# Gathering the first expert pair's tokens by products with the selection matrix, and adding the sample shift on GpSimd

## The chip, the cores and the metric

The kernel runs on one core of a Trainium2 chip, as one launch. The metric is the device time in microseconds; the median of three runs is compared. The engines are PE (TensorE, matrix products), DVE (VectorE), ACT (ScalarE), POOL (GpSimd) and SP (SyncE, which here only issues DMAs).

## The reference, cut to what matters

One decoder layer is computed in float32 for 256 prompt tokens and 8 sample tokens, 1024 features each. The first half (attention, a state space branch, their merge and `w_o`) gives a new `x`. The second half is the one that the change touches:

```python
h2 = rms_norm(x, w['g_norm2']) * (1 + sc2) + sh2
x = x + gt2 * grouped_moe(h2, w_router, b_router, w['w_gate'], w['w_up'], w['w_down'])

def grouped_moe(h, w_router, b_router, w_gate, w_up, w_down):
    logits = (t @ w_router).astype(f32) + b_router.astype(f32)   # 16 experts in 4 groups
    probs = jax.nn.softmax(logits, axis=-1)
    ...                                                          # best group, then top 2 in it
    act = jax.nn.silu(jnp.einsum('td,edf->tef', t, w_gate)) * jnp.einsum('td,edf->tef', t, w_up)
    act = act * comb.astype(act.dtype)[..., None]
    y = jnp.einsum('tef,efd->td', act, w_down)
```

`sc2` and `sh2` (scale and shift) come from the conditions: one pair for all prompt tokens, one for each of the 8 samples. Each expert has three matrices of 1024 x 512 or 512 x 1024 float32, 2.1 MB each.

## The kernel before, in words

The program is written by hand for each engine, with semaphores between them. A list `jobs` sets the order of PE's work for the first half; ACT and DVE walk the same list and read each job's PSUM bank (`filled`, `release`, `read_out`).

Near the end of the list stand the jobs `o` (the product with `w_o`, 8 of them), `lg` (router logits and sums of squares), `hx` and `rk`. `hx` turns the normed features, kept as feature x token, into rows of tokens: three blocks `a` of 128, 128 and 8 tokens (`TOK`), each in two halves `f` of 512 features. ACT copies them out of PSUM with the row's factor `rstd` into `h2tok[a]`, and stores them to DRAM (`h2_d`). The shift of the prompt is added much later, when ACT copies gathered tokens (`gathered`, with bias `shq`). As that adds the prompt's shift to samples too, the rows of the samples must carry the difference of the two shifts, `shrow`. Before the change PE does this: for `a` = 2 it multiplies by `ident` and adds a product of `sdiag` (the deviation on a diagonal) with `shrow` in the same bank. `rk` ranks the tokens of each expert by bf16 products of the assignment, from which DVE's `select` builds the selection matrix `sel` of a pair of experts (264 tokens in three blocks by 128 places, 64 for each expert).

The experts are computed in 8 pairs `j`. For each pair PE gives token numbers (`ids`), from which DVE makes row numbers `idx`; POOL fetches these rows from `h2_d` by an indirect DMA into `xrow` (`fetch`); PE flips them to feature x place (`turn`); ACT copies them to `xg` (`gathered`); then come `gate_up`, `turn_act`, `down` and `combine`. `first_wts` gives the weights of the places for pair 0. `gate_up` has 32 products, in the order gate first half, gate second half, up first half, up second half.

SP streams the expert matrices as 96 halves of 1.05 MB (`load_half(m)`, m = 0 to 95) through 18 places in SBUF. Places 0 to 15 become free during the first half of the layer. Place 16 lies in `attT`, which holds `shrow`, and place 17 in `work`, which holds `h2tok[2]`. From m = 18 on, SP waits until the place of m - 18 is used up (`freed`): `gate_half` for m = 18 and 19, then `gate_done`, `up_half`, `up_done`, `down_half` and `down_done`. SP executes in order, so a wait holds all later loads.

## Time and profile before

| | us |
|---|---|
| median of 3 runs | 853.85 (851.89 to 855.59) |
| the profiled execution's own time | 847.97 |
| its span | 846.4 |
| PE busy | 780.7 (92%) |
| DVE busy | 364.7 (43%) |
| ACT busy | 304.5 (36%) |
| POOL busy | 98.5 (12%) |
| mean DMA rate over the span | 260 GB/s |
| mean granted PE clock | 0.968 of full speed |

### The profile page before, as it was taken

The page shows a single profiled execution, that of the slowest core. Times are in us where ns is not written, and L with a number is a line of the kernel's source. Part 1 is how long each engine was busy: PE and PEld are TensorE (multiplying, and loading weights), DVE is VectorE, ACT ScalarE, POOL GpSimd, SP SyncE. Part 2 cuts the span into 40 slices and gives each one's busy share as a digit, 9 for nine tenths or more (in the row PEclk, how much of TensorE's full clock was granted, in tenths as well). Part 3 has the DMA queues.
Part 4 walks back from the last instruction along what each step waited for, and adds up shares of the span by engine and source line. Part 5 has one row for each costly group of instructions (what it writes and reads, how often), then busy time and mean ns, then how long its engine had stood idle before and what let it go on. Part 6 is the DMA issues. An engine that isn't in the chain of part 4 may idle for free.

```text
span 846.4 us, 12511 instructions
## 1 busy us (share of the span) xinstructions
PE 780.7 (92%) x4573; PEld 546.0 (65%) x4573; DVE 364.7 (43%) x845; ACT 304.5 (36%) x733; POOL 98.5 (12%) x156
## 2 busy tenths in 40 slices
PE   3798979999999899898999999999779999999997
PEld 3375757787776687677887778888534444344434
DVE  3355636675675066375999511112301232222203
ACT  1223216675566256463977100101312222112213
POOL 4321021121200212512001100000010000000000
PEclk9899989999999999999999989999779999999999
DMA  9796353778675712227998995562859999999992
GB/s 294 245 353 216 100 162 118 260 231 299 208 274 180 244 39 78 87 70 212 403 279 255 358 357 183 158 240 100 305 190 423 420 421 420 422 419 421 422 419 97
DMA packets 93532, 219.68 MB, mean 260 GB/s; under 512 B 11792, under 2 KB 67672, under 8 KB 78980
## 3 DMA queue, kind: packets, MB, share of 16 engines
q1 hardware_dynamic: 78850, 181.71, 59.0%
q0 software_dynamic: 7984, 31.87, 11.4%
q10 hardware_dynamic: 6634, 5.25, 2.0%
q8 instruction: 39, 0.64, 0.3%
q14 instruction: 25, 0.20, 0.1%
HBM read 207.58 MB, written 13.22 MB: 261 GB/s over the span
## 4 chain that ended last, share of the span: by engine, by line
PE 66%; DMA 11%; SPq 9%; ACT 5%; DVE 3%; issue 3%; POOL 1%; POOLq 1%; ACTq 0%; DVEq 0%
PE bank L1622 17%; PE bank L1927 9%; PE bank L1848 7%; SPq L549 5%; PE bank L1949 5%; PE bank L1555 4%; DMA out_ssm_sample<-arena 4%; PE bank L1856 4%; PE bank L1618 3%; DMA arena<-in_w_down 3%; PE bank L1830 3%; PE bank L1968 2%; SPq L530 2%; PE bank L1678 2%; DMA out_k_prompt<-arena 1%
## 5 line engine op out<-in xcount | busy, mean ns | idle before, releaser
L1622 PE MATMUL bank<-h_normed,weight_ring 128*128 128x264 f32 x1024 | 243.2, 395 | 10.1 <-ACT arena L894 6.0
L1622 PEld LDWEIGHTS bank<-h_normed,weight_ring 128*128 128x128 f32 x1024 | 195.3, 194 | 48.1 <-ACT arena L894 6.4
L1927 PE MATMUL bank<-arena,h_normed 128*64 128x512 f32 x176 | 79.0, 603 | 0.0
L1848 PE MATMUL bank<-y_T,weight_ring 128*128 128x264 f32 x256 | 58.7, 392 | 0.0
L1927 PE MATMUL bank<-weight_ring,h_normed 128*64 128x512 f32 x192 | 56.3, 594 | 0.6 <-ACT h_normed L1031 0.6
L1848 PEld LDWEIGHTS bank<-y_T,weight_ring 128*128 128x128 f32 x256 | 49.4, 194 | 8.6
L1488 DVE SCALAR_TENSOR_TENSOR x_residual<-bank,modulation,x_residual 128x256 f32<-128x256 f32 x64 | 28.8, 484 | 57.9 <-PE bank L1968 57.9
L1481 DVE TENSOR_TENSOR arena<-arena,bank 128x512 f32<-128x512 f32 x8 | 8.7, 1087 | 104.5 <-PE bank L1927 104.5
L1555 PE MATMUL bank<-identity,arena 128*128 128x128 f32 (+5 forms) x236 | 32.2, 277 | 16.7 <-ACT arena L830 9.3
L1555 PEld LDWEIGHTS bank<-identity,arena 128*128 128x128 f32 (+5 forms) x236 | 26.7, 148 | 27.8 <-issue 22.8
L981 ACT ACTIVATE arena<-conv_out,expanded 128x128 f32<-128x128 f32 x128 | 38.3, 388 | 12.7 <-DVE arena L1364 11.7
L1927 PEld LDWEIGHTS bank<-weight_ring,h_normed 128*64 128x64 f32 x192 | 17.5, 137 | 35.8 <-issue 34.8
L1949 PE MATMUL bank<-arena 128*64 128x512 f32 x88 | 39.2, 595 | 0.0
L799 POOL DMA_INDIRECT h_normed<-h_scratch,token_rows x8 | 8.3, 1033 | 263.5 <-DVE token_rows L1449 143.3
L1287 DVE SCALAR_TENSOR_TENSOR conv_work<-conv_work,vectors 128x288 f32<-128x288 f32 x72 | 37.6, 523 | 2.5
L1031 ACT ACTIVATE h_normed<-bank,conv_tails 128x128 f32<-128x128 f32 x64 | 17.4, 382 | 58.9 <-PE bank L1555 58.9
L1927 PEld LDWEIGHTS bank<-arena,h_normed 128*64 128x64 f32 x176 | 24.1, 139 | 13.8 <-issue 13.8
L1927 PE MATMUL bank<-conv_out,h_normed 128*64 128x512 f32 x64 | 30.0, 621 | 0.3 <-ACT h_normed L1031 0.3
L1856 PE MATMUL bank<-arena,weight_ring 128*128 128x264 f32 x128 | 30.3, 391 | 0.0
L1830 PE MATMUL bank<-att_T,weight_ring 128*128 128x264 f32 x128 | 28.9, 387 | 1.4 <-ACT arena L987 1.4
L1968 PE MATMUL bank<-arena,conv_out 128*128 128x264 f32 x128 | 29.9, 387 | 0.0
L1618 PE MATMUL bank<-h_normed,weight_ring 128*64 128x264 f32 x256 | 29.1, 387 | 0.0
(354 smaller groups left out, 1213.2 us busy)
## 6 DMA issues: line engine op xcount, KB each, us to landing
weight_ring<-in_w_in SPq DMA_DIRECT2D x36, 1024.0 KB, 6.5
weight_ring<-in_w_mod SPq DMA_DIRECT2D x22, 1024.0 KB, 9.3
arena<-in_w_up SPq DMA_DIRECT2D x14, 1024.0 KB, 19.9
weight_ring<-in_w_gate SPq DMA_DIRECT2D x14, 1024.0 KB, 20.0
arena<-in_w_down SPq DMA_DIRECT2D x11, 1024.0 KB, 26.7
weight_ring<-in_w_up SPq DMA_DIRECT2D x10, 1024.0 KB, 18.6
arena<-in_state_ssm POOLq DMA_DIRECT2D x8, 1024.0 KB, 9.1
out_ssm_sample<-arena POOLq DMA_DIRECT2D x8, 1024.0 KB, 9.9
```

The costliest lines, as they stand in the source:

```text
L549: sp.dma_start(half[s], (wg, wu, wdn)[kind][2 * j + e][:, 2048 * h:2048 * h + 2048]).then_inc(moe_full[s // 2], 16)
L981: ins = fn(bx[:, NST * c:NST * c + NST], bc[:, b, 0, :], ACT.Copy, scale=xdt[:, c, b:b + 1])
L1287: link(v.scalar_tensor_tensor(acc, x[:, w:w + XO], vec[:, 104 + 24 * w + i:105 + 24 * w + i], acc, ALU.mult, ALU.add), conv_ready if w == ...
L1555: return tr(out, x, ident[0:k, 0:k])
L1618: ins = mm(ps[64 * x:64 * x + 64, 0:T], slot(s)[:, c, o:o + HD], hT[:, c, :], start=c == 0, stop=c == KD - 1, tile_position=(0, 64 * x))
L1622: ins = mm(ps[:, 0:T], w, hT[:, c, :], start=c == 0, stop=c == KD - 1)
L1830: ins = mm(ps[:, 0:T], slot(s)[:, c, 128 * (i % 2):128 * (i % 2) + 128], attT[:, c, :], start=c == 0, stop=c == KD - 1)
L1848: ins = mm(ps[:, 0:T], w, yT[:, c, :], start=c == 0, stop=c == NXB - 1)
L1856: ins = mm(ps[:, 0:T], slot(s)[:, c, 128 * (i % 2):128 * (i % 2) + 128], gT[:, c, :], start=c == 0, stop=c == KD - 1)
L1927: ins = mm(banks[i][BLK * e:BLK * e + BLK, :], xg[:, 4 * h + c, BLK * e:BLK * e + BLK], ws[e][:, c, :], start=h == 0 and c == 0, stop=h == ...
L1949: ins = mm(banks[2 + q][BLK * e:BLK * e + BLK, :], aT[:, 2 * h + c, BLK * e:BLK * e + BLK], ws[e][:, c, 512 * q:512 * q + 512], start=h == ...
L1968: mm(comb_bank(c)[:, 0:T], outs[:, 128 * c:128 * c + 128], selT[:, j % 2, :], start=True, stop=True)\
```

## The change

Four things are changed together.

- `hx` for the samples (`a` = 2) is now four plain flips for each half, as for the prompt. `sdiag` and its copy on ACT are gone.
- POOL adds `shrow` to the two halves of `h2tok[2]` in SBUF (semaphore `srow_ready`). ACT stores the sample rows after that, behind the exponential of `rk`.
- Pair 0 has no `fetch` and no `turn`. Instead `gather(h)` multiplies the rows `h2tok[a]` (stationary, every eighth column) with `sel[:, a, :]` (moving) and sums over the three blocks, 12 products for each of the two halves. It stands ahead of `ids(0, 0)` on PE. The gate's first half waits for the first half of `xg` only, by a wait moved into the loop.
- The load to place 16 waits for the row stores (`h2_st`), the load to place 17 for `gather` (`xf_filled`).

On PE, the place is from the last `hx` to the first gate product. `conv_out` and `conv_work` hold the token rows, `conv_states` the selection, `conv_tails` the token weights, `att_T` the shift rows. Before:

```order
L1555 MATMUL bank<-identity,h_normed 128x128 x16
L1820 MATMUL bank<-identity,h_normed 8x128
L1821 MATMUL bank<-att_T,conv_tails 8x128
...
L1821 MATMUL bank<-att_T,conv_tails 8x128
L1864 MATMUL bank<-assigned_bf,strict_upper 128x16
...
L1864 MATMUL bank<-assigned_bf,ones_bf 128x16 x3
L1878 MATMUL bank<-conv_tails,conv_states 128x1 x3
L1885 MATMUL bank<-conv_tails,conv_states 128x16 x3
L1555 MATMUL bank<-identity,h_normed 128x128 x8
L1878 MATMUL bank<-conv_tails,conv_states 128x17 x3
L1927 MATMUL bank<-conv_out,h_normed 64x512
```

And now:

```order
L1559 MATMUL bank<-identity,h_normed 128x128 x16
L1559 MATMUL bank<-identity,h_normed 8x128 x8
L1859 MATMUL bank<-assigned_bf,strict_upper 128x16
...
L1859 MATMUL bank<-assigned_bf,ones_bf 128x16 x3
L1909 MATMUL bank<-conv_states,conv_out 128x128 x2
L1909 MATMUL bank<-conv_states,conv_work 128x128
...
L1909 MATMUL bank<-conv_states,conv_work 128x128
L1873 MATMUL bank<-conv_tails,conv_states 128x1 x3
L1880 MATMUL bank<-conv_tails,conv_states 128x16 x3
L1873 MATMUL bank<-conv_tails,conv_states 128x17 x3
L1937 MATMUL bank<-conv_out,h_normed 64x512
```

The 16 products with `sdiag` and the 8 flips of fetched rows are gone, 8 sample flips stand in their place, and 24 gathering products stand between the ranks (L1859) and the first token numbers (L1873).

On POOL, the place is behind the last `iota`. Before:

```order
L789 IOTA conv_tails 128x3 [waits conv_states_stored,pool_step]
L799 DMA h_normed<-h_scratch,token_rows 128x1024 [waits token_row_banks_filled,token_rows_ready,token_numbers_ready,normed_rows_stored]
L799 DMA h_normed<-h_scratch,token_rows 128x1024 [waits token_rows_ready,token_row_banks_filled] x7
```

And now:

```order
L788 IOTA conv_tails 128x3 [waits conv_states_stored,pool_step]
L795 TENSOR_TENSOR conv_work<-conv_work,att_T 8x512 [waits bank_read2,shift_difference_rows_ready,token_numbers_ready]
L795 TENSOR_TENSOR conv_work<-conv_work,att_T 8x512 [waits bank_read3,sample_rows_shifted]
L803 DMA h_normed<-h_scratch,token_rows 128x1024 [waits token_row_banks_filled,token_rows_ready,sample_rows_shifted,normed_rows_stored]
L803 DMA h_normed<-h_scratch,token_rows 128x1024 [waits token_rows_ready,token_row_banks_filled] x6
```

Two additions have come ahead of the fetches, and one fetch is gone.

On SP, the place is the end of the loads that don't wait for the experts' own progress. Before:

```order
L549 DMA arena<-in_w_up 128x2048
L549 DMA att_T<-in_w_down 128x2048 [waits bank_filled3]
L549 DMA conv_work<-in_w_down 128x2048 [waits normed_rows_stored]
L549 DMA conv_out<-in_w_down 128x2048 [waits gate_first_half_used]
L549 DMA arena<-in_w_down 128x2048 [waits gate_first_half_used]
```

And now:

```order
L548 DMA arena<-in_w_up 128x2048
L548 DMA att_T<-in_w_down 128x2048 [waits normed_rows_stored]
L548 DMA conv_work<-in_w_down 128x2048 [waits token_row_banks_filled]
L548 DMA conv_out<-in_w_down 128x2048 [waits gate_first_half_used]
L548 DMA arena<-in_w_down 128x2048 [waits gate_first_half_used]
```

The order is the same; the two waits are others, and `normed_rows_stored` has moved ahead of the 17th load.

The diff:

```diff
--- before.py
+++ after.py
@@ -206,7 +206,6 @@
         rstd = mr[:, 500:503]
         shdiff = mr[:, 504:568].rearrange("p (c b) -> p c b", c=KD)
         shq = mr[:, 568:576]
-        sdiag = mr[0:NS, 576:584]
         past = mr[:, 503:504]
         idx = sb("token_rows", [128, NE // 2], I32)
         asb = sb("assigned_bf", [128, 3, NE], BF16)
@@ -398,7 +397,7 @@
         o_y = sem("y_stored")
         sh_st = sem("prompt_shift_stored")
         shq_in = sem("prompt_shift_landed")
-        sdiag_ready = sem("sample_rms_diagonal_ready")
+        srow_ready = sem("sample_rows_shifted")
         shdiff_rows = sem("shift_difference_rows_ready")
         shdiff_ready = sem("shift_differences_ready")
         gsc_ready = sem("second_gain_ready")
@@ -613,9 +612,9 @@
                 load_expert(n)
             filled_by(("o", 7))
             load_expert(7)
-            filled_by(("hx", 2, 1))
+            sp.wait_ge(h2_st, 48)
             load_half(16)
-            sp.wait_ge(h2_st, 48)
+            sp.wait_ge(xf_filled, 3)
             load_half(17)
             for m in range(NMS, 12 * NPAIR):
                 freed(m - NMS)
@@ -789,6 +788,11 @@
             link(g.iota(tokw[:, :, 0:1], pattern=[[128, 3], [0, 1]], base=1, channel_multiplier=1,
                         allow_small_or_imprecise_dtypes=True), tokrow_ready)
 
+            pool.wait_ge(shdiff_rows, 2)
+            for f in range(2):
+                x = h2tok[2][:, 512 * f:512 * f + 512]
+                read_out(pool, ("hx", 2, f))
+                link(g.tensor_tensor(x, x, shrow[:, 512 * f:512 * f + 512], ALU.add), srow_ready)
             pool.wait_ge(h2_st, 48)
 
             def fetch(r, j):
@@ -799,7 +803,7 @@
                 pool.indirect_dma_start(xrow, None, h2_d, bass.IndirectOffsetOnAxis(idx[:, j:j + 1], 0),
                                         bounds_check=T - 1, oob_is_err=False).then_inc(xr_full, 16)
 
-            for j in range(NPAIR):
+            for j in range(1, NPAIR):
                 fetch(0, j)
             pool.wait_ge(rk_ready, 1)
             rounds = pool.value_load(rounds_sb[0:1, 0:1], min_val=1, max_val=5)
@@ -1011,17 +1015,17 @@
                     a, f, (t0, n) = j[1], j[2], TOK[j[1]]
                     act.wait_ge(rstd_ready, 2)
                     release(act, fn(h2tok[a][:, 512 * f:512 * f + 512], ps[0:n, :], ACT.Copy, scale=rstd[0:n, a:a + 1]), j)
-                    if f == 1:
+                    if f == 1 and a < 2:
                         act.dma_start(h2_d[t0:t0 + n, :], h2tok[a]).then_inc(h2_st, 16)
                 elif k == "lg" and j[1] == KD - 1:
                     act.wait_ge(lg_done, KD)
                     fn(rw[0][:, 0:2], sbank[:, 64:66], ACT.Sqrt, bias=epsc[:], scale=1.0 / D)
                     fn(rw[0][0:NS, 2:3], sbank[0:NS, 66:67], ACT.Sqrt, bias=epsc[0:NS], scale=1.0 / D).then_inc(sd_ready, 1)
-                    act.wait_ge(sd_ready, 1)
-                    fn(sdiag, ident[0:NS, 0:NS], ACT.Copy, scale=rw[0][0:NS, 2:3]).then_inc(sdiag_ready, 1)
                 elif k == "rk":
                     act.wait_ge(d21_ready, 1)
                     fn(rw[5], rw[4], ACT.Exp).then_inc(rk_exp, 1)
+                    act.wait_ge(srow_ready, 2)
+                    act.dma_start(h2_d[NP:T, :], h2tok[2]).then_inc(h2_st, 16)
 
             def gathered(it, h):
 
@@ -1809,17 +1813,8 @@
                     a, f, (t0, n) = j[1], j[2], TOK[j[1]]
                     pe.wait_ge(xgp_ready, 4 * f + 4)
                     pe.wait_ge(xgs_ready, 4 * f + 4)
-                    if a < 2:
-                        for q in range(4):
-                            ins = flip(ps[0:n, 128 * q:128 * q + 128], hT[:, 4 * f + q, t0:t0 + n])
-                    else:
-                        pe.wait_ge(sdiag_ready, 1)
-                        pe.wait_ge(shdiff_rows, 2)
-                        for q in range(4):
-                            c = 4 * f + q
-                            mm(ps[0:n, 128 * q:128 * q + 128], hT[:, c, t0:t0 + n], ident[:], start=True, stop=False)
-                            ins = mm(ps[0:n, 128 * q:128 * q + 128], sdiag, shrow[:, 128 * c:128 * c + 128],
-                                     start=False, stop=True)
+                    for q in range(4):
+                        ins = flip(ps[0:n, 128 * q:128 * q + 128], hT[:, 4 * f + q, t0:t0 + n])
                 elif k == "pa":
                     i = j[1]
                     s = slots_of(j)[0]
@@ -1889,7 +1884,7 @@
 
                 it = r * NPAIR + j
                 if h == 0:
-                    pe.wait_ge(xr_full, (it + 1) * 16)
+                    pe.wait_ge(xr_full, it * 16)
                 pe.wait_ge(xf_read, it * 2 + (h + 1))
                 if j > 2:
                     pe.wait_ge(samp_read, r * (8 * NPAIR) + (8 * (j - 2) + h))
@@ -1900,6 +1895,20 @@
                     ins = flip(banks[5 + h][:, 128 * q:128 * q + 128], xrow.rearrange("s (p k) -> s k p", k=KD)[:, c, :])
                 ins.then_inc(xf_filled, 1)
 
+            def gather(h):
+
+                if h == 0:
+                    pe.wait_ge(sel_ready, 1)
+                    pe.wait_ge(samp_read, 1)
+                    pe.wait_ge(srow_ready, 2)
+                pe.wait_ge(xf_read, h + 1)
+                for q in range(4):
+                    c = 4 * h + q
+                    for a, (t0, n) in enumerate(TOK):
+                        rows = h2tok[a][0:n, :].rearrange("s (p k) -> s k p", k=KD)[:, c, :]
+                        ins = mm(banks[5 + h][:, 128 * q:128 * q + 128], rows, sel[0:n, a, :], start=a == 0, stop=a == 2)
+                ins.then_inc(xf_filled, 1)
+
             def weights(r, j, kind, h):
 
                 ws = []
@@ -1914,13 +1923,14 @@
             def gate_up(r, j):
 
                 it = r * NPAIR + j
-                pe.wait_ge(xf_read, it * 2 + 4)
                 for i, sig in enumerate((gate_done, up_done)):
                     if j > 1:
                         pe.wait_ge(samp_read, r * (8 * NPAIR) + (8 * (j - 2) + 6 + i))
                     elif j == 0:
                         pe.wait_ge(samp_read, it * 8 + 1)
                     for h in range(2):
+                        if i == 0:
+                            pe.wait_ge(xf_read, it * 2 + (3 + h))
                         ws = weights(r, j, i, h)
                         for c in range(4):
                             for e in range(2):
@@ -1970,12 +1980,16 @@
 
             def round_of(r, first=False):
 
+                if first:
+                    gather(0)
+                    gather(1)
                 ids(r, 0)
                 if first:
                     pe.wait_ge(tokw_ready, 1)
                 first_wts(r)
-                turn(r, 0, 0)
-                turn(r, 0, 1)
+                if not first:
+                    turn(r, 0, 0)
+                    turn(r, 0, 1)
                 ids(r, 1)
                 for j in range(NPAIR):
                     gate_up(r, j)
```

## Rows read from the trace of the kernel before

**Rows 1.** Chain that ended last, in order of time: start us, us, what.

```profile
606.90 5.25 DMA h_scratch<-conv_work
...
613.58 4.44 DMA h_normed<-h_scratch,token_rows
...
621.50 15.53 PE bank L1927 x64
...
639.94 13.95 PE bank L1927 x64
...
655.66 7.02 PE bank L1949 x32
...
792.79 26.92 DMA arena<-in_w_down
```

**Rows 2.** SyncE's own instructions: start us, us, DMA issued.

```profile
606.14 0.34 SPq L549 DMA_DIRECT2D att_T<-in_w_down  x1
612.16 0.33 SPq L549 DMA_DIRECT2D conv_work<-in_w_down  x1
626.78 0.33 SPq L549 DMA_DIRECT2D conv_out<-in_w_down  x1
```

**Rows 3.** Windows: stretch, length, busy of PE, PEld, DVE, ACT, POOL, clock, DMA share.

```profile
622.00:624.00 2.00, 2.00 (x6) 0.47 (x4) 1.08 (x5) 0.75 (x1) 1.02 (x1) 0.50 0.00 0
635.00:819.00 184.00, 182.22 (x882) 78.25 (x878) 41.27 (x111) 38.99 (x130) 5.94 (x6) 1.00 1.01 421
```

**Rows 4.** Timeline, 600 to 607 us: start, us, engine, line, what.

```profile
600.77 1.41 ACT L1013 ACTIVATE conv_out<-bank,conv_tails 128x512 f32<-128x512 f32 x2 [0.47 <-PE bank L1555]
...
601.03 0.39 PE L1820 MATMUL bank<-identity,h_normed 128*8 128x128 f32 x2
...
602.21 0.33 ACTq L1015 DMA_DIRECT2D h_scratch<-conv_out  x1
...
602.29 0.21 DVE L1151 TENSOR_TENSOR assigned_bf<-conv_tails 128x48 bf16<-128x48 f32 x1
...
603.64 0.68 ACT L1013 ACTIVATE conv_work<-bank,conv_tails 8x512 f32<-8x512 f32 x1 [1.46 <-PE bank L1821]
...
605.73 0.38 PE L1821 MATMUL bank<-att_T,conv_tails 8*8 8x128 f32 x2
...
606.80 0.21 DVE L1438 SCALAR_TENSOR_TENSOR conv_tails<-bank,conv_tails 128x48 f32<-128x48 f32 x1 [3.87 <-PE bank L1864]
```

**Rows 5.** Timeline, 608 to 622 us, and PE's at 637.97 us.

```profile
608.10 1.50 PE L1878 MATMUL bank<-conv_tails,conv_states 128*128 128x1 f32 x6 [1.42 <-DVE conv_states L1135]
...
611.32 1.57 PE L1885 MATMUL bank<-conv_tails,conv_states 128*128 128x16 f32 x6 [1.72 <-DVE conv_tails L1469]
...
613.35 0.56 DVE L1135 TENSOR_TENSOR conv_states<-slot_numbers,conv_tails 128x384 f32<-128x384 f32 x1
...
619.83 1.41 PE L1878 MATMUL bank<-conv_tails,conv_states 128*128 128x17 f32 x6
...
637.97 0.84 PE L1878 MATMUL bank<-conv_tails,conv_states 128*128 128x17 f32 x6
```

**Rows 6.** GpSimd's groups by line and shape.

```profile
L753 POOL TENSOR_TENSOR arena<-arena,conv_out 128x512 f32<-128x512 f32 x8 | 10.2, 1269 | 27.4 <-ACT arena L955 27.4
```

**Rows 7.** Windows of line 1776 alone: stretch, length, PE and PEld busy, clock, DMA.

```profile
389.25:392.60 3.35, 3.35 (x15) 3.35 (x16) 0.50 0.51 139
392.70:398.20 5.50, 5.50 (x50) 5.36 (x49) 1.00 0.99 267
```

**Rows 8.** The same for line 1927.

```profile
621.50:624.60 3.10, 3.10 (x8) 0.99 (x10) 0.50 0.10 15
```

**Rows 9.** Weight loads of two lines: duration ns min/median/max, first and last start.

```profile
L1555 PEld LDWEIGHTS bank<-identity,h_normed x80: 183/194/231, 597.6 to 788.7; 128*128 128x128 f32 x80
L1555 PEld LDWEIGHTS bank<-identity,conv_out x48: 86/141/144, 296.4 to 331.9; 128*128 128x128 f32 x40, 128*8 128x8 f32 x8
L1776 PEld LDWEIGHTS bank<-arena x64: 191/192/338, 389.2 to 397.9; 128*128 128x128 f32 x64
```

## Prediction

> **What bounds the kernel now.** I read the chain of waits first, then the DMA issues of SyncE and the DMA share by stretches, then the stretch from 597 to 627 us instruction by instruction. In the expert phase the DMA engines are full: from 635 to 819 us their share is 1.02 at 421 GB/s, and the chain ends in the last w_down transfer, which lands at 819.7 us [rows 1, 3]. Just ahead of it the stream stands still: the share is 0.00 from 622 to 624 us [rows 3]. Eighteen half matrices (1.05 MB each) fit before the first pair is computed; the 17th and 18th are issued at 606.14 and 612.16 us, and the next only at 626.78 us, when PE has used the first half of pair 0's gate weights [rows 2]. From there 78 halves remain: 78 x 1.05 MB / 421 GB/s is 194 us, and 626.8 + 194 is 821, near the 819.7 seen. So everything behind 626.78 us is transfer time, and **the one number that counts is when that first half product is done**. One microsecond there is one at the end.
>
> What leads to 626.78 us is this chain: the last sample rows are stored in DRAM (606.90 to 612.15 us), the indirect fetch brings pair 0's rows back (613.58 to 618.02), eight flips and eight ACT copies follow, and the gate product starts at 621.50 us [rows 1]. There PE's granted clock is 0.50 (the lower level, 1.2 GHz), and four steps of two overlapping records take 3.10 us and a little more, some 0.87 us each [rows 8]; pair 1's 64 records, at full clock, take 13.95 us, 0.44 us a step [rows 1]. Four slow and four fast steps are 5.2 of the 5.28 us from 621.50 to 626.78.
>
> **The change, part by part.**
>
> *Removed.* The store and the fetch of pair 0 leave the path: 5.25 + 4.44 us of transfer and 1.4 us of issue between. The store still happens, and the other seven fetches too.
>
> *Sample rows.* Before, 16 products (L1820, L1821) take from 601.03 to 606.03 us, 0.31 us each, at full clock [rows 4]. Now eight plain flips take their place. Even if a flip costs the 0.31 us of the products it replaces, the first four are there at 602.3 us and all at 603.5. ACT has its prompt blocks until 602.18 us and a DMA to issue until 602.54. Its two sample copies of 0.68 us then run from 602.6 to about 604.1 us; before, the first started at 603.64 and the second ended ahead of the store at 606.90 [rows 1, 4]. The small diagonal copy on ACT (0.3 us) goes too, but ACT waited for PE behind it, so I cost it at nothing.
>
> *GpSimd's additions.* The trace has no 8x512 addition on POOL. The nearest is the 128x512 product, 1.27 us [rows 6]. It has the same 512 columns, so I take 1.27, and as the upper bound too, since eight partitions are not more work. The lower bound is DVE's selection, 0.56 us for 384 columns [rows 5], as 0.75 us for 512. The first can start at 603.35 us, so two and a gap of 0.1 end at 606.0 us; at 0.75 us each the second would end at 604.9.
>
> *The route to the selection.* The assignment is there at 602.50 us [rows 4], but the rank products waited behind the 16 products until 606.03 us. They can now start at about 602.6. All that hangs on them moves by the same 3.4 us: DVE's L1438 from 606.80 to 603.4 us, the selection (0.56 us) to 604.3 us. That is ahead of 606.0 us, so the additions decide when the gathering starts, and slower flips or rank products have 1.7 us of cover.
>
> *The gathering.* 24 products of 128 columns, 48 records on PE, as each plain f32 product here is two. Two thirds have the form of L1776 (128x128 by 128x128), one third K=8. L1776 gives both prices: 15 records in 3.35 us at clock 0.50 (0.22 us each), then 50 in 5.50 us at 1.00 (0.11 us) [rows 7]. Those products stood alone as these do, started at half clock and rose. I let the gathering do the same: 15 records in 3.35 us and 33 x 0.11 = 3.6 us, **7.0 us, to 613.0 us**. The bounds are 48 x 0.11 = 5.3 us and 48 x 0.22 = 10.6 us; as three operand heights alternate, the dearer row is L1820/L1821 with 0.31 us for a product that alternates K=128 and K=8 at full clock, which is 7.4 us for 24, and if that doubles at half clock, 14.9 us.
>
> *What comes behind it on PE's queue.* The engine executes in order, and the gathering stands ahead of the first token numbers (L1878), so all small steps that used to hide under the store and the fetch are now behind it: the numbers, 0.84 us at full clock (the row at 637.97) or 1.50 at half (608.10); DVE's way from there to the weights, 609.60 to 611.32 us, 1.7 us; the weight products 1.57 us at half clock; DVE's copies and the next selection, 612.89 to 613.91 us, 1.0 us; the numbers of pair 1, 1.41 us at half clock [rows 5]. I take full clock for the first, as it follows the dense gathering, and half for the other two, as PE rests around them: 613.0 + 0.84 + 1.7 + 1.57 + 1.0 + 1.41 = **619.5 us**. ACT's eight copies of gathered rows lie under this, as the second half is in PSUM 6.5 us before. The gate product thus starts 2.0 us earlier than at 621.50, not the 11 us of the path removed.
>
> *The gate's first half* costs 5.28 us as before: 624.8 us instead of 626.78.
>
> *The two held loads.* The 17th half now waits until the third row store has landed, the 18th until the gathering is done, and on SP's queue every later load stands behind them. The store was issued at 606.9 and landed at 612.15 us; now it is issued near 606.3, behind the exponential on ACT. The 18th would go out at 613.0 us and take 2.5 us and a latency. The first use of either is the down product at 655.66 us [rows 1], and the loads behind them wait for 624.8 us anyway. Cost nothing; the cover is 12 us on SP and 38 us on PE.
>
> *Sum.* 626.78 - 624.8 = 2.0 us less. The profiled execution had a span of 846.4 us and a time of 847.97 us, so it would be near 846.0 us; the median of the runs shown is 853.85 us, 0.7% above that execution, and becomes **851.8 us**. That is 0.23%; about 0.5% (4.3 us) is what a measurement of this kernel can tell from no change.
>
> **A rule against it.** The stationary operand of the gathering takes every eighth float of a row. The loads of h_normed, 64 of 80 of them with that stride, have a median of 194 ns; those of conv_out, without it, 141 ns; but the loads of L1776, without it, have 192 ns and still give 0.11 us a record [rows 9]. So the rows leave it open, and rather speak against a cost. The Trainium skill (SBUF — State Buffer, Door 1: The DMA port swizzle) says that accesses which step past a 16-byte line pay a penalty each. As a mechanism here: if each record is bound by its load and loads stretch by 194/141 = 1.38, the records take 0.30 and 0.15 us, 11 of them in the half-clock 3.35 us and 37 x 0.15 = 5.6 us, 8.9 us in all. The gain is then 0.1 us: 853.7 us.
>
> **The rivals.**
> - *As summed*, with the clock coming and going as above: 851.8 us, own range 850 to 853. Chance 0.47.
> - *PE stays at full clock.* For it: PE is dense from 606 us on, where it waited for the fetch. Then 606.0 + 5.3 + 0.84 + 1.7 + 0.84 + 1.0 + 0.84 = 616.5 us, and the gate's eight steps at 0.44 us take 3.5 us: 620.0 us, 6.8 us less, 847.1 us. Against it: two DVE stretches of 1.7 and 1.0 us, and tiny products between, and the same work ran at the lower level in the trace, 1.50 us for six records where 0.84 is the price at full clock. With faster additions half of it would still come. Chance 0.20.
> - *The strided loads cost*: 853.7 us. Chance 0.13.
> - *The gathering runs wholly at half clock*: 10.6 us, 1.50 for the numbers, so 623.8 us and 629.1 us: 2.3 us more, 856.2 us. Chance 0.10.
> - *Slower*: alternating K=128 and K=8 breaks the overlap of loads and products as in L1820/L1821, and at half clock: 606.0 + 14.9 + 1.50 + 1.7 + 1.57 + 1.0 + 1.41 + 5.28 = 633.4 us, 6.6 us more, 860.5 us. It decides from a gathering of 12.6 us on, 0.26 us a record. Against it: the numbers of pair 2 have the same mix and take 0.84 us for six records. Chance 0.07.
> - *The earlier start does not reach the end*, because something else holds the stream: 853.9 us. Against it: a share of 0.00 before and 1.02 behind. Chance 0.03.
>
> **How the numbers follow.** The likeliest is 851.8 us. The range of 847.0 to 856.3 us leaves out the slower case (0.07), about half of the second (0.10) and the edges of the others: it holds about 0.8. Faster by over 0.5% needs 4.3 us: most of the second case and a tail of the first, 0.23. Slower by over 0.5%: the fifth case and a tail of the fourth, 0.08. Within: 0.69.
>
> **What would show it.** ACT's sample copies end near 604.0 us, the second addition near 606.0; the gathering takes about 7 us; the gate starts near 619.5 and SyncE's 19th load goes out near 624.8 us (all counted from an assignment at 602.50 us). I am wrong if the additions take under 0.5 us each, if the gathering is over 9 us, if the clock is 1.00 while the gate starts, or if DMA share under 0.9 appears behind the 19th load.

## The result, and the profile after

The changed kernel takes 858.24 us (median of 12 runs, 854.22 to 863.78), the kernel before 851.61 us (12 runs beside them, 847.06 to 855.59). The ratio is 1.0084, 95% interval 1.0053 to 1.0115: 0.84% slower, where 0.2% faster was forecast. It lies above the range.

From here on the **local stretch** is the time from the first token flip to SyncE's 19th load (m = 18). Before, it goes from 597.56 us to 626.78 us, 29.2 us [rows 2]. The page of the changed kernel, first the span, then engine busy, granted clock and DMA rate in 40 slices:

```profile
span 860.7 us, 12550 instructions
PE 790.6 (92%) x4589; PEld 553.3 (64%) x4589; DVE 365.8 (42%) x845; ACT 304.3 (35%) x732; POOL 100.0 (12%) x157
PEclk9999989999999999999999999999569999999999
GB/s 293 246 352 199 108 161 136 249 223 324 184 270 200 187 58 59 101 77 301 319 259 237 371 376 167 151 196 123 269 114 421 420 423 419 422 420 421 422 420 100
```

PE's busy time rose by 10 us, and it did so in the local stretch (31.9 us there for 20.7). The clock digits 5 and 6 of slices 29 and 30 and the rate of 114 GB/s in slice 30 are that stretch, the hole ahead of the expert stream. Behind it the stream is as full as before, as the windows show (stretch, length, busy of PE, PEld, DVE, ACT, POOL, clock, DMA share, GB/s):

```profile
611.60:627.90 16.30, 16.25 (x49) 12.70 (x49) 0.00 (x0) 1.14 (x4) 0.00 (x0) 0.50 0.34 128
627.90:635.20 7.30, 4.50 (x18) 4.19 (x18) 2.29 (x12) 2.42 (x5) 0.00 (x0) 0.50 0.44 144
635.20:639.60 4.40, 4.40 (x13) 1.31 (x14) 1.73 (x10) 0.00 (x0) 1.11 (x1) 0.50 0.12 20
650.00:833.00 183.00, 181.61 (x880) 77.92 (x876) 41.33 (x111) 38.99 (x130) 5.97 (x6) 1.00 1.01 421
```

The last row answers to 1.01 and 421 GB/s of [rows 3]. The chain of waits of the changed kernel, in order of time, answers to [rows 1]:

```profile
602.16 1.90 PE bank L1559 x8
...
607.15 0.69 ACT conv_work L1017
...
608.00 1.26 POOL conv_work L795
...
609.33 1.47 POOL conv_work L795
610.82 0.29 ACTq L1028
...
611.65 16.24 PE bank L1909 x48
627.89 1.47 PE bank L1873 x6
...
631.06 1.58 PE bank L1880 x6
...
633.71 1.57 PE bank L1873 x6
635.28 16.09 PE bank L1937 x64
```

One row holds most of the loss: the gathering takes 16.24 us, not 7.0. SyncE's loads, which answer to [rows 2]:

```profile
614.91 0.33 SPq L548 DMA_DIRECT2D att_T<-in_w_down  x1
627.92 0.33 SPq L548 DMA_DIRECT2D conv_work<-in_w_down  x1
641.11 0.33 SPq L548 DMA_DIRECT2D conv_out<-in_w_down  x1
```

The first token flip is at 602.08 us in this execution (4.5 us later than in the one of before, as work further up, which the change does not touch, scatters between executions: in the runs below that flip lies between 596.5 and 603.1 us). The local stretch is 641.11 - 602.08 = 39.0 us, 9.8 us more than before. From the 19th load to the end of the span it is 219.6 us in both kernels.

Inside the gathering, PE and its weight loads, from the timeline:

```profile
611.62 1.03 PEld L1909 LDWEIGHTS bank<-conv_states,conv_out 128*128 128x128 f32 x4 [3.92 <-issue]
612.88 0.55 PEld L1909 LDWEIGHTS bank<-conv_states,conv_work 8*128 8x128 f32 x2 [0.22 <-issue]
613.65 1.04 PEld L1909 LDWEIGHTS bank<-conv_states,conv_out 128*128 128x128 f32 x4 [0.22 <-issue]
```

A chunk (two blocks of 128 rows and one of 8, six records) takes 613.65 - 611.62 = 2.03 us, eight of them the 16.24. Each time the operand changes between 128 and 8 rows, the weight loads pause for 0.22 us, and the granted clock is 0.50 throughout, as the first window shows. Counted from start to start, a load follows the one before it after 0.22 to 0.24 us, and after 0.56 us where the height changes: some 0.32 us more, fifteen times, or 4.8 us.

### The profile page after: what moved, and what is told of

Read it like the earlier page. It is cut to its first block, busy times and chain, and to the rows that moved or that the text cites. A ratio compares the mean times of both kernels' runs of the same rounds, so it can differ in the third digit from the quotient of the medians.

```text
span 860.7 us, 12550 instructions
## 1 busy us (share of the span) xinstructions
PE 790.6 (92%) x4589; PEld 553.3 (64%) x4589; DVE 365.8 (42%) x845; ACT 304.3 (35%) x732; POOL 100.0 (12%) x157
## 4 chain that ended last, share of the span: by engine, by line
PE 66%; DMA 11%; SPq 6%; ACT 5%; DVE 4%; issue 3%; ACTq 2%; POOL 1%; POOLq 1%; DVEq 0%
PE bank L1626 16%; PE bank L1937 8%; PE bank L1843 7%; SPq L548 6%; PE bank L1559 4%; PE bank L1959 4%; DMA out_ssm_sample<-arena 4%; PE bank L1851 3%; PE bank L1622 3%; DMA arena<-in_w_down 3%; PE bank L1825 3%; PE bank L1580 2%; PE bank L1909 2%; PE bank L1978 2%; PE bank L1682 2%
## 5 line engine op out<-in xcount | busy, mean ns | idle before, releaser
L1978 PE MATMUL bank<-arena,conv_out 128*128 128x264 f32 x128 | 29.9, 387 | 0.0
L1368 DVE SCALAR_TENSOR_TENSOR arena<-arena,sample_decays 128x1024 f32<-128x1024 f32 x16 | 19.9, 1282 | 20.4 <-ACT arena L985 16.7
## 6 DMA issues: line engine op xcount, KB each, us to landing
arena<-in_w_up SPq DMA_DIRECT2D x14, 1024.0 KB, 20.7
```

The source lines that it names most:

```text
L1978: mm(comb_bank(c)[:, 0:T], outs[:, 128 * c:128 * c + 128], selT[:, j % 2, :], start=True, stop=True)\
```

## The experiments

The theory after the result was this: two things of the gathering's operands cost, the changes of height (128, 128, 8 rows) and the stride of the stationary one, and the low clock comes with them. The rivals: it is the clock alone; it is the order on PE's queue; it is the sample part on ACT and GpSimd. Twelve kernels were run, in four groups, each beside runs of the kernel before (medians 850.9, 850.7, 850.9 and 851.6 us). The code below shows the main lines of each edit.

The local stretch and the gathering are those of the one profiled execution of each kernel, the ratio is that of all its runs. The gathering goes up to the start of PE's next step; for after, e1 and e3 it is the chain's piece, which is up to 0.2 us longer.

| run | median us | ratio to before (95%) | local stretch us | gathering us |
|---|---|---|---|---|
| before | 851.61 | 1 | 29.2 | none |
| after | 858.24 | 1.0084 (1.0053 to 1.0115) | 39.0 | 16.24 |
| e1 | 847.87 | 0.9971 (0.9928 to 1.0014) | 29.0 | 7.89 |
| e2 | 857.31 | 1.0084 (1.0049 to 1.0119) | 37.3 | 15.0 |
| e3 | 856.23 | 1.0059 (1.0029 to 1.0090) | 35.5 | 12.57 |
| e4 | 856.55 | 1.0069 (1.0034 to 1.0104) | 35.7 | 16.16 |
| e5 | 852.01 | 1.0019 (0.9987 to 1.0051) | 30.7 | none |
| e6 | 852.97 | 1.0026 (0.9996 to 1.0057) | 32.9 | 11.5 |
| e7 | 857.42 | 1.0080 (1.0046 to 1.0114) | 38.8 | 15.7 |
| e8 | 848.09 | 0.9990 (0.9961 to 1.0020) | 29.2 | 11.6 |
| e9 | 851.67 | 0.9998 (0.9972 to 1.0024) | 29.9 | 8.3 |
| e10 | 844.36 | 0.9946 (0.9917 to 0.9976) | 25.9 | 7.1 |
| e11 | 845.40 | 0.9935 (0.9908 to 0.9961) | 23.7 | 7.1 |
| e12 | 841.26 | 0.9870 (0.9838 to 0.9903) | 21.5 | 5.5 |

**e1, without the sample block's products.**

```diff
-                    for a, (t0, n) in enumerate(TOK):
+                    for a, (t0, n) in enumerate(TOK[0:2]):
...
-                        ins = mm(banks[5 + h][:, 128 * q:128 * q + 128], rows, sel[0:n, a, :], start=a == 0, stop=a == 2)
+                        ins = mm(banks[5 + h][:, 128 * q:128 * q + 128], rows, sel[0:n, a, :], start=a == 0, stop=a == 1)
```

> Leaves out the third product of each chunk (the 8 sample rows), so samples sent to pair 0 get no features. In the changed kernel the gathering took 16.2 us for 48 records at half clock: 0.31 us for a record of 128 rows and 0.38 for one of 8. Theory A (each change between operand heights of 128 and 8 rows breaks the overlap of load and product): without changes 32 records at 0.22 us, 7.0 us, 9 us less; if the clock rises meanwhile, 5 to 6. Theory B (the strided stationary operand makes the load slow): 32 x 0.31 = 10 us, 6 us less. From the first token flip to SyncE's 19th load: 39.0 us in the changed kernel, 30 by A, 33 by B. The end moves with it: 9 or 6 us faster than the changed kernel.

The 32 records that are left take 7.89 us, 0.25 us each, so 16 records with 8 rows cost 8.35 us of the 16.24. But 0.25 us a record is far above 0.11, and it stays so where the clock was up. The two windows below are of the gathering alone; by the weight loads, the chunks of four records start 0.96 us apart in the first and 0.95 us apart in the second, 0.24 us a record in both.

```profile
606.75:611.40 4.65, 4.65 (x19) 4.65 (x20) 0.50 0.67 260
611.50:614.70 3.20, 3.14 (x14) 2.95 (x13) 1.00 0.83 302
```

**e2, neighbouring columns instead of every eighth** (pair 0 gets its features in another order than its weights have).

```diff
-                        rows = h2tok[a][0:n, :].rearrange("s (p k) -> s k p", k=KD)[:, c, :]
+                        rows = h2tok[a][0:n, 128 * c:128 * c + 128]
```

> The stationary operand takes 128 neighbouring floats of each row and not every eighth, so pair 0 gets its features in another order than its weights have; the work is the same. Theory A (height changes): the gathering stays at 16.2 us at half clock. Theory B (stride): the 32 records of 128 rows go from 0.31 to 0.22 us, 13.3 us, 3 us less, and the kernel 3 us faster than the changed one.

15.0 us at clock 0.50 throughout: 1.2 us less. The stride alone explains little as long as the heights alternate, here at clock 0.50.

**e3, products grouped by height**: for each half all of block 0, then 1, then the samples (the start flags, left at each block's first product of every chunk, drop part of the sums of pair 0's prompt tokens).

```diff
-                for q in range(4):
-                    c = 4 * h + q
-                    for a, (t0, n) in enumerate(TOK):
+                for a, (t0, n) in enumerate(TOK):
+                    for q in range(4):
+                        c = 4 * h + q
```

> The same 24 products, but for each half first the four of block 0, then the four of block 1, then the four of the samples: 3 height changes in place of 15. Theory A: 32 x 0.22 + 16 x 0.22 + 3 x 0.5 = 12 us at half clock, 4 us less than 16.2, and 4 us faster at the end; if the denser stream lifts the clock on the way, 8 to 10 us. Theory B: 16 us, unchanged.

```profile
605.95 4.18 PE L1909 MATMUL bank<-conv_states,conv_out 128*128 128x128 f32 x16 [3.73 <-ACTq L1069]
```

3 changes of height in place of 15 take the gathering to 12.57 us. The 16 records of 128 rows above take 0.26 us each, and their loads start 0.24 us apart, as in e1; the clock was up only from 610.35 to 613.76 us.

**e4, the first token numbers ahead of the gathering.**

```diff
+                ids(r, 0)
                 if first:
                     gather(0)
                     gather(1)
-                ids(r, 0)
```

> The token numbers of pair 0 stand ahead of the gathering on PE and no longer behind it; PE idles there anyway for the additions, and DVE's way to the weights then lies under the gathering. Theory C (order on PE's queue): the gathering still takes 16.2 us, but 1.5 us of numbers and 1.7 us of DVE leave the path, the gate starts 3.2 us earlier, 35.8 us from the first flip to the 19th load instead of 39.0. Rival: the gathering starts later by the numbers' 1.5 us, and only 1.7 us or nothing is won.

The gathering stays at 16.16 us, and the local stretch falls by 3.3 us, as the numbers and DVE's way to the weights now lie under other work. The order is a real term, but a third of the loss.

**e5, the sample part alone**, pair 0 fetched and flipped as before.

```diff
-            for j in range(1, NPAIR):
+            for j in range(NPAIR):
                 fetch(0, j)
...
-                if first:
-                    gather(0)
-                    gather(1)
...
-                if not first:
-                    turn(r, 0, 0)
-                    turn(r, 0, 1)
+                turn(r, 0, 0)
+                turn(r, 0, 1)
```

> One part alone: the sample rows are made as in the changed kernel (plain flips, additions on GpSimd, store behind them), but pair 0 is fetched from DRAM and flipped as before. From the first token flip to SyncE's 19th load the kernel before took 29.2 us. The second addition ended 8.7 us behind the first flip in the changed kernel, and the store of before was issued at 9.3 us. Theory D (the sample part is worth the earlier store): the store goes out 0.6 us earlier, and as it no longer stands among the 17th load's packets it lands 1 to 2 us earlier: 27.5 to 28.5 us, 1 to 2 us faster than before. Rival: the additions cost as much as the products did, and it is the kernel before within noise, 29 us.

The store goes out earlier, but the local stretch is 1.5 us longer than before. The chain shows why:

```profile
607.24 4.68 DMA h_scratch<-conv_work
...
613.37 7.44 DMA h_normed<-h_scratch,token_rows
```

The fetch took 4.44 us before [rows 1] and takes 7.44 now: SyncE's 17th and 18th loads wait for the same store and go out at 611.94 and 612.32 us, 2.1 MB ahead of the fetch in the 16 engines. Before, only the 18th stood there, issued at 612.16 us, 1.4 us ahead of the fetch as the two are here [rows 1, 2]. One load more is 1.05 MB / 421 GB/s = 2.5 us by my estimate, near the 3.0 us lost; no run moved that load alone, so this cause is likely, not shown.

**e6, the sample block padded to 128 rows** (120 rows of zeros, zeroed once by GpSimd, 0.95 us at 497.41 us, so that every operand has 128 rows; nothing is left out).

```diff
-                    for a, (t0, n) in enumerate(TOK):
-                        rows = h2tok[a][0:n, :].rearrange("s (p k) -> s k p", k=KD)[:, c, :]
+                    for a in range(3):
+                        rows = blocks[a].rearrange("s (p k) -> s k p", k=KD)[:, c, :]
```

> The sample block is padded with zero rows to 128, so that all 24 products have one operand height; the result stays the reference's. Theory A (height changes): the 48 records take 0.22 us each at half clock, 10.6 us, and as the stream is dense the clock comes up in it, as without the sample block: 7 to 9 us instead of 16.2, and 7 to 9 us faster than the changed kernel, about the time of the kernel before. Theory B2 (the number of records is what costs, whatever their height): 16 us as in the changed kernel.

More rows, less time: 11.5 us for the same 48 records, 4.7 less. So the changes of height cost, not the small operand. What is left does not follow the clock. Windows of the gathering alone:

```profile
611.00:616.20 5.20, 5.20 (x22) 5.20 (x23) 0.50 0.72 247
616.20:622.50 6.30, 6.30 (x28) 6.28 (x27) 1.00 0.39 148
```

0.24 us a record at 0.50 and the same at 1.00 (chunks of six records start 1.44 and 1.43 us apart), with PEld busy all the time, and at a DMA share of 0.72 and of 0.39 alike. The 4.7 us are what the fifteen pauses added up to above (4.8 us). The expectation of 7 to 9 us was missed, as the records did not follow the clock when it rose.

**e7, four unused products of 512 columns in PE's wait**, to keep the clock up.

```diff
+            for i in range(4):
+                mm(sbank[:, 0:512], onesf[:], hT[:].rearrange("p c t -> p (c t)")[:, 0:512], start=True, stop=True)
```

> The changed kernel with four idle products of 512 columns (results unused) on PE between the ranks and the gathering, where PE waits for the additions. They take 3.4 us at full clock, as long as the wait. Theory E (the half clock is due to that wait): the clock is 1.00 when the gathering starts, and with 0.11 us a record and 0.22 us for each of 15 height changes it takes 8 to 9 us, 7 us less, and the kernel is 7 us faster than the changed one. Rival: the alternating products let the clock fall again, and 2 to 4 us are won; or none.

The clock was up when the gathering began, and fell back at 611.83 us, within it. A chunk takes 1.79 us at 1.00 and 2.03 at 0.50, so at full clock all through I estimate 8 x 1.79 = 14.3 us. The clock alone is thus ruled out as the cause.

**e8, four things together**: e6's padding, the numbers first as in e4, blocks 0 and 1 gathered for all chunks ahead of the sample block (one start flag a bank), and ACT's three counter increments at the start of its program.

```diff
+                if first:
+                    for a in range(3):
+                        gather(a)
```

> Padded sample block, the token numbers ahead of the gathering, all products of blocks 0 and 1 ahead of those of the sample block, so that only the latter wait for the additions, and ACT's first increments of its counters at its program's start and not behind the store. The result stays the reference's. With theories A and C: gathering from 8.0 to 17 us behind the first flip, weights 1.6, DVE 1.0, numbers 1.5, so the gate starts at 21 us and the 19th load goes out at 26 us, 3 us earlier than in the kernel before: 848 us where before has 851. By the rivals B2 it would stay behind the kernel before, at 33 us.

The local stretch is 29.2 us, that of before, and not the 26 us expected; 11.6 us of it are the 48 records, still 0.24 us each at either clock.

**e9, padded and with neighbouring columns** (pair 0's features in another order, as in e2).

```diff
-                        rows = blocks[a].rearrange("s (p k) -> s k p", k=KD)[:, c, :]
+                        rows = blocks[a][:, 128 * c:128 * c + 128]
```

> This is e6 (sample block of 128 rows, the lower 120 zero) with one thing more: each gathering product reads 128 neighbouring columns of the token rows in place of every eighth, so pair 0 gets its features in another order than the weights have. In e6 a record took 0.24 us at clock 0.50 and at 1.00 alike, and the 48 took 11.5 us. Theory S (a strided stationary load holds a record at 0.24 us, whatever the clock): now 0.22 us a record at 0.50 and 0.11 at 1.00, as L1776 before; if the clock rises 5.3 us after the start as in e6, 24 records at 0.22 and 24 at 0.11, so 7.9 us for the 48 and 29.3 us from the first token flip to SyncE's 19th load (e6: 32.9), near 849.5 us. Theory M (something else than the stride, such as the change of bank or of the moving block, holds it): 0.24 us a record stays, 11.5 us, near 853 us.

```profile
610.20:616.20 6.00, 6.00 (x28) 6.00 (x29) 0.50 0.68 231
616.20:618.50 2.30, 2.30 (x22) 2.25 (x21) 1.00 0.88 356
```

0.21 us a record at 0.50 (6.00 us for 28) and 0.11 at 1.00 (chunks of six start 0.67 us apart), the prices of [rows 7]. Theory S holds: with 128 rows everywhere, the stride is what kept a record at 0.24 us when the clock rose.

**e10, e8 with the stride moved off PE's loads** (nothing left out).

```diff
-                    release(act, fn(h2tok[a][:, 512 * f:512 * f + 512], ps[0:n, :], ACT.Copy, scale=rstd[0:n, a:a + 1]), j)
+                    release(act, fn(half_row(h2tok[a], f), ps[0:n, :].rearrange("s (g k) -> s g k", k=KD), ACT.Copy,
+                                    scale=rstd[0:n, a:a + 1]), j)
```

> This is e8 with the stride moved away from PE: ACT writes the token rows and the shift rows in the order of the chunks (a strided write), so that the gathering and the later flips of fetched rows read 128 neighbouring columns; GpSimd adds in runs of 64 columns and waits for DVE's selection first. Nothing of the computation is left out. e8 took 11.6 us for the gathering and 29.24 us from first flip to 19th load. Theory S (the stride holds the record at 0.24 us): gathering 7.9 us, local 25.5 us, near 844.5 us, a ratio of 0.993 to the kernel before. Theory M: 11.6 us stays, near 848. A way in which both are too low: ACT's strided copies take over 0.69 us each, or GpSimd's additions over 1.3 us each, since they now wait for the selection.

The gathering takes 7.1 us, and this is the first version faster than the kernel before, at 0.9946. The timeline shows the price of the move, 1.14 us a copy instead of 0.70, and that the sample block is not waited for:

```profile
603.80 2.27 ACT L1032 ACTIVATE conv_work<-bank,conv_tails 8x512 f32<-8x512 f32 x2 [0.48 <-ACT conv_out L1032]
605.09 2.59 POOL L802 TENSOR_TENSOR conv_work<-conv_work,att_T 8x512 f32<-8x512 f32 x2 [110.94 <-ACT conv_work L1032]
606.38 1.49 PE L1886 MATMUL bank<-conv_tails,conv_states 128*128 128x1 f32 x6 [3.41 <-ACT conv_work L1032]
607.81 5.52 PE L1922 MATMUL bank<-conv_states,conv_out 128*128 128x128 f32 x32
613.16 1.95 PE L1922 MATMUL bank<-conv_states,conv_work 128*128 128x128 f32 x16
```

**e11, e10 with three unused products** (two behind the ranks, one behind the first weights).

```diff
+            busy(2, sbank)
...
                 first_wts(r)
+                if first:
+                    busy(1, banks[2])
```

> This is e10 with three products of 512 columns whose result nothing uses: two behind the rank products, one behind the first token weights, so that PE rests less. If the clock stays at 1.00 through the gathering, it takes 48 x 0.11 = 5.3 us, the token numbers 0.84 us for 1.5, and the gate's first half 3.5 for 5.3 or so: 2 to 4 us less than e10. Rival: e7's way, the clock falls back all the same, and the unused products only stand in front of the numbers: 0 to 1.5 us more than e10.

The local stretch is 2.2 us shorter: the numbers take 0.88 us for 1.49, and from 616.28 us on the clock stays up, so that the gate's first half takes 3.6 us for 5.3. The clock fell back as the gathering began (0.50 from 612.86 to 616.28 us), and the gathering is no shorter, where 5.3 us was expected. Between the whole times of e10 and e11 (0.9946 and 0.9935, the intervals overlap) no difference can be told.

**e12, e11 with the features put in order by the token flips' output** instead of by ACT's copies.

```diff
-                        ins = flip(ps[0:n, 128 * q:128 * q + 128], hT[:, 4 * f + q, t0:t0 + n])
+                        ins = flip(ps[0:n, :].rearrange("s (k q g) -> s q g k", k=KD, q=4)[:, q], hT[:, 4 * f + q, t0:t0 + n])
```

> This is e11 with the reordering of the features moved from ACT's copies to the output of the token flips: each flip writes its 128 columns into the PSUM bank as 16 runs' places of 8 chunks, and ACT copies runs of 64 columns. Nothing of the computation is left out. In e10 and e11 ACT's six copies of token rows take 1.14 us each, and the numbers start when the last is read (606.38 us in e10, copies ending 606.09), where the plain copies took 0.69. If PE's scattered PSUM writes cost nothing, the copies take 0.7 us each, the six end some 2 us earlier and the local stretch is 21.7 us for e11's 23.7, near 843 us. If the flips pay for the scattered writes (over 0.3 us each where they take 0.19 now), or ACT still takes 1.1 us a copy since it is the runs that cost, the local stretch stays at 23.7 us or grows.

```profile
603.12 2.84 PE L1572 MATMUL bank<-identity,h_normed 128*128 128x128 f32 x24
604.10 1.41 ACT L1032 ACTIVATE conv_out<-bank,conv_tails 128x512 f32<-128x512 f32 x2 [0.48 <-DVE conv_tails L1447]
...
612.71 3.84 PE L1928 MATMUL bank<-conv_states,conv_out 128*128 128x128 f32 x32
616.38 1.95 PE L1928 MATMUL bank<-conv_states,conv_work 128*128 128x128 f32 x16
```

The 24 flips take 2.84 us at full clock, just what e9's plain ones take, and ACT's copies are back at 0.70 us. The gathering, at full clock throughout here, takes 5.5 us for 48 records. With a ratio of 0.9870 this is the fastest kernel of the study. The local stretch explains 2.2 us of the distance to e11; the rest of it (e11 was timed in another group of runs) isn't settled.

The 21.5 us are close to the 21.7 expected, but by luck, as they came another way. ACT's last copy ends 6.1 us behind the first flip, 2.9 us earlier than in e11, and yet the numbers start only 0.5 us earlier (8.85 us for 9.33). The two unused products hold PE until then, at clock 0.50 from 608.13 to 611.55 us. The chain:

```profile
608.87 3.26 PE bank L1880 x4
```

And the timeline, with the copies of the samples and the numbers:

```profile
607.87 1.39 ACT L1032 ACTIVATE conv_work<-bank,conv_tails 8x512 f32<-8x512 f32 x2 [0.48 <-ACT conv_out L1032]
611.97 0.81 PE L1892 MATMUL bank<-conv_tails,conv_states 128*128 128x1 f32 x6
```

The other 1.6 us are the gathering, 5.5 us for 7.1, since the clock was back at 1.00 before it began. That e12's own change brings the clock is not shown, and e12 without these two products was not run.

In the profiled executions of all fourteen kernels, 219.3 to 220.5 us lie between the 19th load and the end of the span, so what the local stretch gains or loses reaches the end there. The ratios follow it more loosely: e3 +6.3 us local and +5.0 by its ratio, e4 +6.5 and +5.9, e2 +8.1 and +7.1, e6 +3.6 and +2.2, e10 -3.4 and -4.6, after +9.8 and +7.2, e7 +9.6 and +6.8, e12 -7.7 and -11.1. The uncertainty of a ratio is some 3 us each way; e12 lies outside it, and the local stretch itself is read from one execution of each kernel.

## Why the prediction was wrong, step by step

On the scale of the kernel before (4.5 us taken off each time of after):

- *What bounds the kernel* was right: the 19th load's time decides, and 219.6 us follow it in both. (The share of 1.02 that I quote is 1.01 in [rows 3].)
- *Sample copies and additions* were right: the copies end at 604.0 us (604.1 forecast), GpSimd's additions take 1.26 and 1.47 us (1.27 each), end 606.3 (606.0).
- *The selection* takes 1.52 us, not 0.56, and still ends 1.1 us ahead of the additions. In e10, where GpSimd waits for it, it takes 0.56 us again, so the two get in each other's way. The Trainium skill (SBUF — State Buffer, SBUF: two separate sides) says that GpSimd and an operation of DVE with two SBUF inputs lock a shared pair of ports for a whole instruction; the trace agrees, as the selection, started 0.15 us behind the first addition (608.00 to 609.26 us), ends 0.4 us after it. It cost nothing here, as the additions ended later.
- *The start of the gathering* was 0.85 us late: its waits include counters that ACT increments in its queue only behind the store of the sample rows (the chain from 610.82 to 611.65). I had left that wait out. It was hidden before by the fetch. No run moves these counters alone, so 0.85 us is the most that they cost.
- **The gathering's price is the step that failed**: 7.0 us forecast, 16.24 measured, 9.2 of the 11.8 us between forecast and result. I took the price from L1776 [rows 7], whose products have one height and no stride. Both differences cost. The change of height was my rival "slower" (14.9 us, 860.5 us, chance 0.07); I had set it aside because of the numbers' six records in 0.84 us, which change height once, not fifteen times. The pause is in that very row: its loads start at 637.97, 638.08, 638.19 and, behind the change of height, 638.41 us. From the runs, one way of splitting the 16.24: 4.7 us go with the padding (e6), 3.2 more with the stride (e9, 8.3 us), 2.8 more with the clock (e12, 5.5 us). It is not a sum of independent parts: with alternating heights the stride is worth only 1.2 us (e2) and the clock 1.9 by the estimate from e7.
- *The rule against it* was set aside for a wrong reason. [rows 9] compares loads of flips, and a strided flip in fact costs hardly more: the eight flips of pair 1's fetched rows take 1.16 us strided in the changed kernel and 1.09 us dense in e10, 0.14 us each. For plain float32 products the stride costs: 0.24 us a record against 0.11 at full clock (e6, e9). The Trainium skill (SBUF — State Buffer, Door 1: The DMA port swizzle) speaks of a penalty for accesses past a 16-byte line; the direction agrees, and the size here, a factor of 2.2 at clock 1.00 and 1.1 at 0.50, is not the 1.38 that I had worked out.
- *The clock* was to rise after 3.35 us of gathering. It stayed at 0.50 until 639.7 us, so the numbers and small steps behind the gathering took 7.3 us (6.5 forecast) and the gate's first half 5.9 (5.28).
- *The order on PE's queue* was seen rightly and costed a little low: 2.5 us for the numbers and DVE's way to the weights, and e4 shows 3.3 us by moving one line. The remaining 2.6 of the 11.8 us are such small parts: 0.3 us in the additions, 0.85 in the start, 0.8 and 0.6 in the steps at the lower clock.
- *The held loads* cost nothing here, as forecast. In e5, where the fetch stays and both loads stand ahead of it, the fetch takes 3 us longer.

## What to carry to other kernels

A price per record holds only for its operand's height, stride and clock: before a DMA is replaced by products, look for a row with the same three, and let the range go to the worst of them where there is none. Pad short blocks to the full height where they alternate with full ones, keep the stationary operand of a plain float32 product dense, and put a reordering where it is free (here the PSUM output of a flip). When a long wait is taken out, list all that it covered: here a queue order worth 3.3 us and a counter worth up to 0.85.

## What the runs showed that was not expected

- A change of the stationary operand's height between 128 and 8 rows stops the weight loads for 0.22 us (0.56 us from start to start for 0.24 at clock 0.50, 0.45 in e7 at 1.00); 48 records fell from 16.24 to 11.5 us by adding 120 rows of zeros.
- A stationary load with a stride of eight floats holds a plain float32 record at 0.24 us at clock 0.50 and 1.00 alike; a flip of the same stride pays under 0.01 us (1.16 us for eight against 1.09), and a flip with a scattered PSUM output nothing that shows.
- ACT's copy of 512 columns from PSUM takes 1.14 us where single floats are written in another order, and 0.70 us where runs of 64 are, as much as a plain one.
- The same indirect fetch took 7.44 us behind two loads of 1.05 MB, and 4.44 us behind one.
